# Token tables of the gates from two rounded one-hot products, with the low part of the gate made by ScalarE

## The chip, the cores and the metric

The kernel runs on one NeuronCore of a Trainium2 chip. TensorE (PE) multiplies, and its weight loads are shown as PEld; VectorE (DVE), ScalarE (ACT) and GpSimd (POOL) work beside it; SyncE (SP) issues most DMAs. Each engine runs its own list of instructions strictly in the order of the program and waits on semaphores where the program says so. The metric is the device time of one execution in microseconds (us), less is better.

## The reference

One transformer-like layer over 512 tokens of width 1024: a gated mix of attention and convolution, and then a retrieval (PEER) from a table of 128 x 128 = 16384 experts. All inputs are float32. The change lies in the second half:

```
q = (hf @ w_q).reshape(T, PEER_HEADS, 2, PEER_DHALF)
scores = einsum('thpd,pnd->thpn', q, sub_keys)          # 128 first and 128 second keys
sv, si = top_k(scores, 16)
cand = sv[:, :, 0, :, None] + sv[:, :, 1, None, :]
cv, ci = top_k(cand, 16)                                 # 8 heads x 16 = 128 slots a token
e_idx = si0[ia] * 128 + si1[ib]
gates = softmax(cv)
a = einsum('thkd,td->thk', u_tab[e_idx], x)
out = einsum('thk,thkd->td', gelu(a) * gates, v_tab[e_idx])
```

## The kernel before

The kernel does not gather the expert rows of three of its four tiles of 128 tokens. It multiplies all 16384 rows of `u_tab` with these 384 tokens (the first product, 128 chunks of 128 experts), takes gelu of everything, multiplies by a dense table of gates that is zero for experts a token did not choose, and multiplies by all of `v_tab` (the second product). Matrices are split into a rounded high part and a low part, both of type fp32r, and each product is three matmuls (`three`, lines 1785 to 1787): high by high, low weight by high, high weight by low.

The dense table of gates has one 128 x 128 matrix for each token: entry (second key, first key). For tile 1 it is filled by 128 scattering DMAs of GpSimd (line 727). For two further tiles (`LAID` = 2) it is made on chip, a token at a time, as a product of one-hot matrices over the token's 128 slots: `one_hots` (lines 1620 to 1635) makes for `WIDE` = 8 tokens at once, a set, a matrix that is 1 where the slot's first key equals the column, one for the second key, and multiplies the latter by the slot's gate. That is three DVE instructions of 128 x 1024 a set, 16 sets a tile. `token_gates` (line 2065) then issues a plain float32 matmul a token, four tokens to a group (`TOK` = 4), two groups to a set, into bank 2 or 3. The profile shows each such float32 matmul as two instructions, so a group as x8. ACT copies each bank into `stage` (`gates`, line 972), and every eighth copy a DMA writes `stage` to memory.

All of this is laid beside the first product. A step is one chunk of it: 8 units of three matmuls on PE. Tile by tile there are four stages of 14, 14, 26 and 26 steps (`STEPS`); the last two, which this text calls stage 3 and stage 4, carry the token tables of the two tiles. In them PE issues group b before unit `GATE_UNIT[b]`, that is from step 4 on, one every 5.5 units, 32 groups a stage; a set is used every 11 units, or 1.375 steps.

What each engine does in its order in one step:

- ACT (`selecting` at line 989, `ahead` at line 965): gelu of the chunk just multiplied (line 963), the high part `whi` of the chunk after the next (line 952, three buffers `SPL`), then the copies of those groups that belong to this step (line 981).
- DVE (`select`, line 1505): the search for the next tile (top 16, candidates, sums), and between its parts (`beside`) the low parts `wlo` of the chunks (line 1467) and the sets. The table `LOWS` says how many low parts come at each point, and a set comes before a low part as soon as `KD * (made[0] - 1) // 11` allows it.
- POOL: the scatters and, for a few chunks a stage (`SEARCHING`), the low part in place of DVE (line 717).
- PE: the first product of chunk c waits for its low part and for the gelu of chunk c - 2; a group waits for its set (`one_r`) and for the copy of the group two before it (`gt_sb`).

A set may overwrite its buffer once the groups of the set `BUFS` earlier are multiplied (`gt_mm`); there are four buffers of 8 KB.

Of the kernel before, what the change touches and what calls it, by code (L numbers as in the profile page):

```python
# [5 lines left out]
F32 = mybir.dt.float32  # L6
F32R = mybir.dt.float32r
I32 = mybir.dt.int32
U32 = mybir.dt.uint32
ALU = mybir.AluOpType  # L10
ACT = mybir.ActivationFunctionType
AX = mybir.AxisListType.X

P = 128
D = 1024
T = 512
KD = D // P
TT = T // P
# [8 lines left out]
NK = 128  # L27
# [60 lines left out]
WIDE = 8  # L88
# [65 lines left out]
LOWS = ((1, 1, 1, 1, 1, 1, 1, 1, 1, 1, 1, 1, 0, 1, 0, 1), (1, 3, 3, 2, 2, 2, 2, 1, 1, 1, 1, 1, 1, 1, 1, 3))  # L154

LAID = TD - 1
BUFS = 4
SEL_UNIT, GATE_LEAD = 12, 4
GATE_UNIT = [KD * GATE_LEAD + b * KD * (STEPS[2] - GATE_LEAD) // NBT for b in range(NBT)]
EXP_STEP = (11, 11, 22, 22)  # L160
# [6 lines left out]
def build(nc, x, cb, ccol, w_modn, b_modc, w_modt, wblk, b_fc, conv_wc, conv_vec, keys_t, u_t, u_tab, v_tab, rows, out):  # L167
    with ExitStack() as ctx:
# [3 lines left out]
        def sb(name, shape, dt, kb):  # L172
            return nc.alloc_sbuf_tensor_at(name, shape, dt, offset=base + int(kb * KB))

        def sem(name):
            return ctx.enter_context(nc.semaphore(name))

        bank = [ctx.enter_context(nc.psum_tensor(f"bank{i}", [P, 512], F32)) for i in range(8)]
# [46 lines left out]
        stage = sb("stage", [P, 2, NK, TB], F32, 120)  # L225
        eq = sb("eq", [P, 2, TOPK * NCAND], F32, 192)
        selT = sb("selT", [P, 3, P], F32, 199)
        one = [sb(f"one{i}", [P, 2, WIDE, NK], F32, 152 + 8 * i) for i in range(BUFS)]
        selS = sb("selS", [P, SLOTS], I32, 190)
        selW = sb("selW", [P, SLOTS], F32, 190.5)  # L230
        zeros = sb("zeros", [P, HALF], F32, 132)
# [157 lines left out]
        selT_mm = sem("selT_mm")  # L389
        selT_sb = sem("selT_sb")  # L390
        one_r = sem("one_r")
        zero_r = sem("zero_r")
        zero_out = sem("zero_out")
        gate_add = sem("gate_add")
# [30 lines left out]
        class Chain:  # L425
# [5 lines left out]
            def link(self, ins):  # L431
                self.n += 1
                ins.then_inc(self.s, 1)
                self.eng.wait_ge(self.s, self.n)
# [329 lines left out]
        def _(act):  # L764
# [45 lines left out]
            for n in range(G0):  # L810
                if n > 1:
                    hi(n + 2)
                if n >= Q0:
                    act.wait_ge(blk_mm, n + 1)
                    dst = qa if n < K0 else ka
                    for r in range(2):
                        ins = nc.scalar.activation(dst[0:DH, 2 * ((n - Q0) % 4) + r, :],
                                                   bank[z_bank[n]][r * DH:(r + 1) * DH, :], ACT.Copy,
                                                   scale=-DH ** -0.5 if n < K0 else 1.0)
# [145 lines left out]
            def ahead(c):  # L965

                if c:
                    gelu(c - 1)
                if c + 2 < CH:
                    part_u(c + 2)  # L970

            def gates(l, b):
# [11 lines left out]
                if t0 == TB - TOK:  # L984
                    act.wait_ge(gt_sb, n + 1)
                    act.dma_start(gates_dram[:, :, P // TB + blk, :],
                                  stage[:, s].rearrange("p (q f) t -> p q (f t)", f=4)).then_inc(stage_out[s], 16)

            def selecting(s):
                for j in range(STEPS[s]):  # L990
                    ahead(S_AT[s] + j)
                    if j == EXP_STEP[s]:
                        act.wait_ge(gate_sub, s + 1)
                        nc.scalar.activation(sel[:, 1, :, :], cv[:], ACT.Exp).then_inc(gate_exp, 1)
                    if s >= TT - LAID:
                        for b in range(NBT):
                            if GATE_UNIT[b] // KD == j:
                                gates(s - TT + LAID, b)
# [65 lines left out]
        def _(dve):  # L1064
# [544 lines left out]
            def transposed(s):  # L1609

                dve.wait_ge(selT_mm, s)
                nc.vector.tensor_copy(selT[:, 2, :], bank[2][:, P:2 * P])
                link(nc.vector.tensor_copy(selI[:, 0, :], bank[2][:, 0:P]))
                link(nc.vector.tensor_scalar(selI[:, 1, :], selI[:, 0, :], NK - 1, None, ALU.bitwise_and))
                link(nc.vector.tensor_scalar(selI[:, 0, :], selI[:, 0, :], NK.bit_length() - 1, None,
                                             ALU.logical_shift_right))
                link(nc.vector.tensor_copy(selT[:, 0:2, :], selI[:]))
                nc.vector.nop().then_inc(selT_sb, 1)

            def one_hots(l, o):  # L1620

                shape = [P, WIDE, NK]
                n = P // WIDE * l + o
                if n == 0:
                    dve.wait_ge(xs_r, 2)
                need(dve, gt_mm, 2 * (n - BUFS) + 2)
                row = one[n % BUFS]
                part = slice(o * WIDE, (o + 1) * WIDE)
                keys_of = iota[:].unsqueeze(1).broadcast_to(shape)
                link(nc.vector.tensor_tensor(row[:, 1], selT[:, 0, part].unsqueeze(2).broadcast_to(shape), keys_of,  # L1630
                                             ALU.is_equal))
                nc.vector.tensor_tensor(row[:, 0], selT[:, 1, part].unsqueeze(2).broadcast_to(shape), keys_of,  # L1632
                                        ALU.is_equal)
                nc.vector.tensor_tensor(row[:, 1], row[:, 1], selT[:, 2, part].unsqueeze(2).broadcast_to(shape),  # L1634
                                        ALU.mult).then_inc(one_r, 1)

            nc.vector.tensor_scalar(tokI[:, 1:2], tokI[:, 1:2], TB.bit_length() - 1, None, ALU.logical_shift_right)
# [142 lines left out]
        def _(pe):  # L1780
# [284 lines left out]
            def token_gates(l, b):  # L2065

                n = NBT * l + b
                pe.wait_ge(one_r, n // 2 + 1)
                need(pe, gt_sb, n - 1)
                if b == 0:  # L2070
                    pe.wait_ge(selT_sb, l + 1)
                row = one[n // 2 % BUFS]
                for j in range(TOK):
                    i = n % 2 * TOK + j
                    last = mm(bank[2 + b % 2][:, j * NK:(j + 1) * NK], row[:, 0, i, :], row[:, 1, i, :],  # L2075
                              start=True, stop=True)
                last.then_inc(gt_mm, 1)

            def selecting(s):
# [105 lines left out]
```

## Time and profile before

| | |
|---|---|
| median of three runs | 1624.3 us (1623.93 to 1624.91) |
| profiled execution, its own time | 1621.99 us |
| its span | 1620.2 us |
| PE busy, weight loads busy | 1554.3 us (96%), 1358.6 us (84%) |
| DVE, ACT, POOL busy | 1361.3 us (84%), 679.4 us (42%), 680.6 us (42%) |
| chain that ended last | PE 61%, DVE 26%, DMA 7%, issue 4%, ACT 1% |
| matmuls of the token tables (line 2075) | x512, 276 ns each |
| sets (lines 1630, 1632, 1634) | 32 of each, 1.2 us each where nothing disturbs |

Stage 3 lies between about 579 us and 725 us of the span (the transposes of line 2062 stand at 579.0 and 724.8 us), stage 4 behind it until about 862 us. Matmuls and ACT instructions overlap their neighbours, so the distance between two starts says what one costs, and its duration is longer than that. A wait is printed in brackets behind the instruction that waited, with the work that released it.

### The profile page before, as it was taken

How to read it: one execution, taken by the hardware profiler on the slowest of the kernel's cores; microseconds unless marked ns; L12 is line 12 of the kernel's file. 1: busy time of each engine (PE TensorE's matmuls, PEld its weight loads, DVE VectorE, ACT ScalarE, POOL GpSimd, SP SyncE). 2: the span in 40 equal slices, each digit the busy share in tenths (PEclk: the TensorE clock that was granted, in tenths of full speed). 3: DMA queues.
4: the chain of work that ended last, by engine and by line, in shares of the span. 5: the costliest groups of instructions: out<-in, count | busy, mean ns of one | idle time of the engine just before them, and what ended most of it. 6: DMA issues, size and time to landing. Idle time of an engine off the chain costs nothing.

```text
span 1620.2 us, 21549 instructions
## 1 busy us (share of the span) xinstructions
PE 1554.3 (96%) x7772; PEld 1358.6 (84%) x7772; DVE 1361.3 (84%) x2603; ACT 679.4 (42%) x923; POOL 680.6 (42%) x445
## 2 busy tenths in 40 slices
PE   5999999997999999999999999999999899999997
PEld 3888777776899999999999999999988688877775
DVE  6579887797288899979994888888878899999998
ACT  4344656435334344555554433333323333333341
POOL 0201000000043778777864455565553555555511
PEclk9999999998999999999999999999999999999998
DMA  9423444562367657686868999999989999999981
GB/s 365 145 90 118 130 130 130 195 208 78 119 228 251 170 146 182 153 236 169 217 183 285 411 395 350 373 356 365 342 296 372 401 409 409 409 409 408 409 328 52
DMA packets 162489, 422.17 MB, mean 261 GB/s; under 512 B 31568, under 2 KB 64464, under 8 KB 162128
## 3 DMA queue, kind: packets, MB, share of 16 engines
q1 hardware_dynamic: 72288, 264.44, 44.6%
q0 software_dynamic: 57200, 139.58, 25.4%
q10 hardware_dynamic: 32896, 16.78, 3.7%
q8 instruction: 62, 1.02, 0.2%
q14 instruction: 43, 0.35, 0.1%
HBM read 375.55 MB, written 45.15 MB: 260 GB/s over the span
## 4 chain that ended last, share of the span: by engine, by line
PE 61%; DVE 26%; DMA 7%; issue 4%; ACT 1%; SPq 0%; DVEq 0%; ACTq 0%
PE bank L1785 18%; PE bank L1787 18%; PE bank L1786 18%; DVE acc L1703 6%; DMA vraw<-in_v_tab_dram 6%; DVE one L1632 2%; DVE wf L1658 2%; DVE one L1630 2%; DVE wlo L1467 2%; DVE one L1634 2%; DVE el L1665 2%; PE bank L2075 1%; PE bank L1931 1%; PE bank L1916 1%; PE bank L2051 1%
## 5 line engine op out<-in xcount | busy, mean ns | idle before, releaser
L1785 PE MATMUL bank<-act_hi,whi 128*128 128x384 f32 (+1 forms) x1352 | 480.7, 356 | 3.6 <-DVE act_lo L1181 2.1
L1787 PE MATMUL bank<-act_hi,wlo 128*128 128x384 f32 (+1 forms) x1352 | 472.0, 349 | 0.0
L1786 PE MATMUL bank<-act_lo,whi 128*128 128x384 f32 (+1 forms) x1352 | 471.8, 349 | 0.0
L1785 PE MATMUL bank<-vhi,eh 128*128 128x512 f32 x768 | 302.6, 394 | 15.2 <-DVE el L1665 15.0
L1787 PE MATMUL bank<-vhi,el 128*128 128x512 f32 x768 | 301.3, 392 | 0.0
L1786 PE MATMUL bank<-vlo,eh 128*128 128x512 f32 x768 | 301.2, 392 | 0.0
L1785 PEld LDWEIGHTS bank<-act_hi,whi 128*128 128x128 f32 x1352 | 255.1, 189 | 20.6 <-DVE act_lo L1181 3.6
L1786 PEld LDWEIGHTS bank<-act_lo,whi 128*128 128x128 f32 x1352 | 255.2, 189 | 13.7
L727 POOL DMA_INDIRECT gates_by_key<-selW,selS x128 | 237.7, 1857 | 67.3 <-issue 46.3
L1787 PEld LDWEIGHTS bank<-act_hi,wlo 128*128 128x128 f32 x1352 | 254.7, 188 | 13.3
L750 POOL DMA_INDIRECT ring<-in_v_tab_dram,idxN x128 | 185.9, 1452 | 174.5 <-DVE acc L1703 136.3
L711 POOL DMA_INDIRECT ring<-in_u_tab_dram,idxN x128 | 178.0, 1391 | 150.8 <-DVE ring L1472 107.1
L1670 DVE TENSOR_TENSOR vlo<-vraw,vhi 128x1024 fp32r<-128x1024 f32 x128 | 156.2, 1221 | 65.7 <-ACT vhi L1024 65.4
L1024 ACT ACTIVATE vhi<-vraw 128x1024 fp32r<-128x1024 f32 x128 | 134.9, 1055 | 129.5 <-PE bank L1787 109.2
L1467 DVE TENSOR_TENSOR wlo<-raw,whi 128x1024 fp32r<-128x1024 f32 x108 | 131.9, 1222 | 66.5 <-ACT whi L952 66.0
L1785 PEld LDWEIGHTS bank<-vhi,eh 128*128 128x128 f32 x768 | 145.2, 189 | 50.7 <-issue 22.0
L1011 ACT ACTIVATE eh<-wf 128x384 fp32r<-128x384 f32 x128 | 67.4, 526 | 281.8 <-DVE wf L1658 275.9
L1787 PEld LDWEIGHTS bank<-vhi,el 128*128 128x128 f32 x768 | 145.2, 189 | 30.9
L1786 PEld LDWEIGHTS bank<-vlo,eh 128*128 128x128 f32 x768 | 145.3, 189 | 29.6 <-issue 0.2
L1703 DVE SCALAR_TENSOR_TENSOR acc<-ring,own_a,acc 128x1024 f32<-128x1024 f32 x127 | 162.7, 1281 | 5.4 <-DVE acc L1703 0.5
L1472 DVE SCALAR_TENSOR_TENSOR ring<-ring,x2s 128x1024 f32<-128x1024 f32 x128 | 149.9, 1220 | 0.7 <-DMA ring<-in_u_tab_dram,idxN 0.7
L963 ACT ACTIVATE gelz<-bank 128x384 f32<-128x384 f32 x128 | 63.3, 495 | 179.6 <-PE bank L1787 177.1
(256 smaller groups left out, 1964.7 us busy)
## 6 DMA issues: line engine op xcount, KB each, us to landing
raw<-in_u_t_dram SPq DMA_DIRECT2D x128, 512.0 KB, 7.2
vraw<-in_v_tab_dram SPq DMA_DIRECT2D x128, 512.0 KB, 10.8
raw<-in_wblk_dram SPq DMA_DIRECT2D x61, 512.0 KB, 4.4
gring<-gates_by_key SPq DMA_DIRECT2D x32, 768.0 KB, 12.0
raw<-in_w_modt_dram SPq DMA_DIRECT2D x32, 512.0 KB, 3.7
gates_by_key<-stage ACTq DMA_DIRECT2D x8, 2048.0 KB, 13.9
gelu_ahead<-gelz SPq DMA_DIRECT2D x20, 768.0 KB, 4.2
gback<-gelu_ahead SPq DMA_DIRECT2D x40, 384.0 KB, 17.7
```

What stands on the lines that cost most here:

```text
L711: pool.indirect_dma_start(out=ring[:, j % RING, :], out_offset=None, in_=u_tab, in_offset=bass.IndirectOffsetOnAxis(ap=idxN[:, j:j + 1], a ...
L727: pool.indirect_dma_start(out=gates_flat, out_offset=bass.IndirectOffsetOnAxis(ap=selS[:, n:n + 1], axis=0), in_=selW[:, n:n + 1], in_offs ...
L750: pool.indirect_dma_start(out=ring[:, j % RING, :], out_offset=None, in_=v_tab, in_offset=bass.IndirectOffsetOnAxis(ap=idxN[:, j:j + 1], a ...
L1011: nc.scalar.activation(e_parts(n)[0], wf[:, n % 2, :], ACT.Copy).then_inc(w_hi, 1)
L1024: nc.scalar.activation(v_parts(n)[0], row, ACT.Copy).then_inc(v_hi, 1)
L1467: nc.vector.tensor_tensor(wlo[:, c % SPL, :], raw[:, c % RAW, :], whi[:, c % SPL, :].bitcast(F32), ALU.subtract).then_inc(u_lo, 1)
L1472: nc.vector.scalar_tensor_tensor(out=ring[:, j % RING, :], in0=ring[:, j % RING, :], scalar=1.0, in1=x2s[:], op0=ALU.mult, op1=ALU.mult, a ...
L1670: nc.vector.tensor_tensor(low, v_row(n)[0], high.bitcast(F32), ALU.subtract).then_inc(v_lo, 1)
L1703: nc.vector.scalar_tensor_tensor(out=acc[:, TD, :], in0=ring[:, j % RING, :], scalar=own_a[:, j:j + 1], in1=acc[:, TD, :], op0=ALU.mult, o ...
L1785: mm(o, wh, mh, start=start, stop=False)
L1786: mm(o, wh, ml, start=False, stop=False)
L1787: return mm(o, wl, mh, start=False, stop=stop)
```

## The change

- DVE now writes the two one-hots of a set as fp32r (`one_a`, `one_b`), and a third tile `one_g`, the second one-hot times the high part of the gate. There are still three DVE instructions a set.
- ACT makes the fourth tile in place: `low_gates` multiplies `one_b` by the low part of the gate, one instruction of 128 x 128 for each of the 8 tokens, with the token's column of `selT` as a scale operand. It counts `one_lo`. It stands in ACT's order right after `ahead`, in the step before the one in which the set is first used.
- The high and the low part of the gates are made once a tile in `transposed`: a copy to fp32r and a subtraction in place of one copy.
- PE waits for `one_lo` in place of `one_r`, and issues two fp32r matmuls of 128 columns a token, which add up in the bank.
- A set is 12 KB in place of 8 KB, and there are two buffers in place of four.

```diff
-BUFS = 4
+BUFS = 2
...
+            def low_gates(l, o):
+                n = P // WIDE * l + o
+                act.wait_ge(one_r, n + 1)
+                for i in range(WIDE):
+                    token = o * WIDE + i
+                    last = nc.scalar.activation(one_b[n % BUFS][:, i, :], one_b[n % BUFS][:, i, :].bitcast(F32), ACT.Copy,
+                                                scale=selT[:, 2, token:token + 1])
+                last.then_inc(one_lo, 1)
+
             def selecting(s):
                 for j in range(STEPS[s]):
                     ahead(S_AT[s] + j)
+                    if s >= TT - LAID:
+                        for o in range(P // WIDE):
+                            if GATE_UNIT[2 * o] // KD - 1 == j:
+                                low_gates(s - TT + LAID, o)
...
-                nc.vector.tensor_copy(selT[:, 2, :], bank[2][:, P:2 * P])
+                link(nc.vector.tensor_copy(gate_hi[:], bank[2][:, P:2 * P]))
+                nc.vector.tensor_tensor(selT[:, 2, :], bank[2][:, P:2 * P], gate_hi[:].bitcast(F32), ALU.subtract)
...
                 need(dve, gt_mm, 2 * (n - BUFS) + 2)
-                row = one[n % BUFS]
...
-                link(nc.vector.tensor_tensor(row[:, 1], selT[:, 0, part].unsqueeze(2).broadcast_to(shape), keys_of,
+                link(nc.vector.tensor_tensor(one_b[n % BUFS][:], selT[:, 0, part].unsqueeze(2).broadcast_to(shape), keys_of,
                                              ALU.is_equal))
-                nc.vector.tensor_tensor(row[:, 0], selT[:, 1, part].unsqueeze(2).broadcast_to(shape), keys_of,
+                nc.vector.tensor_tensor(one_a[n % BUFS][:], selT[:, 1, part].unsqueeze(2).broadcast_to(shape), keys_of,
                                         ALU.is_equal)
-                nc.vector.tensor_tensor(row[:, 1], row[:, 1], selT[:, 2, part].unsqueeze(2).broadcast_to(shape),
+                nc.vector.tensor_tensor(one_g[n % BUFS][:], one_b[n % BUFS][:].bitcast(F32),
+                                        gate_hi[:, part].bitcast(F32).unsqueeze(2).broadcast_to(shape),
                                         ALU.mult).then_inc(one_r, 1)
...
-                pe.wait_ge(one_r, n // 2 + 1)
+                pe.wait_ge(one_lo, n // 2 + 1)
...
-                    last = mm(bank[2 + b % 2][:, j * NK:(j + 1) * NK], row[:, 0, i, :], row[:, 1, i, :],
-                              start=True, stop=True)
+                    mm(bank[2 + b % 2][:, j * NK:(j + 1) * NK], one_a[k][:, i, :], one_g[k][:, i, :], start=True, stop=False)
+                    last = mm(bank[2 + b % 2][:, j * NK:(j + 1) * NK], one_a[k][:, i, :], one_b[k][:, i, :],
+                              start=False, stop=True)
```

How the instructions stand on ACT at steps 3 to 6 of stage 3, before (gelz is a gelu, whi a high part, stage the copy of a group):

```order
L963 ACTIVATE gelz<-bank 128x384
L952 ACTIVATE whi<-raw 128x1024
L963 ACTIVATE gelz<-bank 128x384
L952 ACTIVATE whi<-raw 128x1024
L981 ACTIVATE stage<-bank 128x4x128 x2
L963 ACTIVATE gelz<-bank 128x384
L952 ACTIVATE whi<-raw 128x1024
L981 ACTIVATE stage<-bank 128x4x128
L963 ACTIVATE gelz<-bank 128x384
L952 ACTIVATE whi<-raw 128x1024
L981 ACTIVATE stage<-bank 128x4x128 x2
```

And now (the eights on one_b are the low parts of sets 0, 1 and 2):

```order
L967 ACTIVATE gelz<-bank 128x384
L956 ACTIVATE whi<-raw 128x1024
L998 ACTIVATE one_b_101<-one_b_101,selT 128x128 x8
L967 ACTIVATE gelz<-bank 128x384
L956 ACTIVATE whi<-raw 128x1024
L998 ACTIVATE one_b_102<-one_b_102,selT 128x128 x8
L985 ACTIVATE stage<-bank 128x4x128 x2
L967 ACTIVATE gelz<-bank 128x384
L956 ACTIVATE whi<-raw 128x1024
L998 ACTIVATE one_b_101<-one_b_101,selT 128x128 x8
L985 ACTIVATE stage<-bank 128x4x128
```

The low part of set 1 now stands ahead of the copies of the first two groups, and that of set 2 ahead of the copy of the third; nothing else moved.

On DVE the same place, after the change (two sets, a low part of a chunk, a part of the search, a set); before, the three rows of a set stand at the same places with `one` in place of the three names:

```order
L1647 TENSOR_TENSOR one_b_102<-selT,iota 128x1024
L1649 TENSOR_TENSOR one_a_100<-selT,iota 128x1024
L1651 TENSOR_TENSOR one_g_104<-one_b_102,gate_hi 128x1024
L1647 TENSOR_TENSOR one_b_101<-selT,iota 128x1024
L1649 TENSOR_TENSOR one_a_99<-selT,iota 128x1024
L1651 TENSOR_TENSOR one_g_103<-one_b_101,gate_hi 128x1024
L1484 TENSOR_TENSOR wlo<-raw,whi 128x1024
L1505 MATCH_REPLACE sc_94<-both_of,bank 128x128 x16
L1647 TENSOR_TENSOR one_b_102<-selT,iota 128x1024
```

The low part `wlo` right behind set 2 (the second set shown) is that of chunk 8 of the stage, whose high part ACT makes in step 6.

## Rows read from the trace of the kernel before

**Rows 1.** Part 1 of the page: engine, busy us, share, instructions.

```profile
PE 1554.3 (96%) x7772; PEld 1358.6 (84%) x7772; DVE 1361.3 (84%) x2603; ACT 679.4 (42%) x923; POOL 680.6 (42%) x445
```

**Rows 2.** Windows in stage 3: length, then busy of PE, PEld, DVE, ACT, POOL; clock.

```profile
592.00:640.00 48.00, 46.20 (x297) 45.28 (x296) 47.54 (x115) 25.23 (x29) 39.47 (x20) 1.00 0.65 175
640.00:690.00 50.00, 49.37 (x315) 48.63 (x315) 47.46 (x126) 24.63 (x28) 40.43 (x22) 1.00 0.69 164
690.00:724.00 34.00, 32.65 (x209) 32.33 (x208) 25.99 (x38) 19.91 (x24) 22.89 (x14) 1.00 0.84 241
```

**Rows 3.** Waits, 575 to 862 us: who for whom; total us, times, longest.

```profile
ACT stage L981 <- PE bank L2075: 82.9, 45, 5.1
DVE wlo L1467 <- ACT whi L952: 18.9, 11, 3.8
PEld bank L2075 <- DVE one L1634: 8.3, 8, 2.3
```

**Rows 4.** Timeline of PE around one group: start, us, engine, line, operands.

```profile
589.34 0.33 PE L1785 MATMUL bank<-act_hi,whi 128*128 128x384 f32 x1
589.69 0.33 PE L1787 MATMUL bank<-act_hi,wlo 128*128 128x384 f32 x1
589.86 1.05 PE L2075 MATMUL bank<-one 128*128 128x128 f32 x8
590.93 0.34 PE L1786 MATMUL bank<-act_lo,whi 128*128 128x384 f32 x1
```

**Rows 5.** Weight loads by form (count, busy, mean ns), and eight on the timeline.

```profile
L1787 PEld LDWEIGHTS bank<-act_hi,wlo 128*128 128x128 f32 x1352 | 254.7, 188 | 13.3
L1931 PEld LDWEIGHTS bank<-probT,vals 128*64 128x64 f32 x64 | 8.1, 136 | 12.8 <-issue 7.6 <-ACT probT L845 3.9
...
20.33 0.97 PEld L1881 LDWEIGHTS bank<-strips,mrows 128*128 128x128 f32 x8
```

**Rows 6.** Timeline of ACT in stage 3.

```profile
590.45 1.05 ACT L952 ACTIVATE whi<-raw 128x1024 fp32r<-128x1024 f32 x1
...
601.32 0.49 ACT L963 ACTIVATE gelz<-bank 128x384 f32<-128x384 f32 x1 [1.49 <-PE bank L1787]
601.71 1.05 ACT L952 ACTIVATE whi<-raw 128x1024 fp32r<-128x1024 f32 x1
602.65 1.13 ACT L981 ACTIVATE stage<-bank 128x512 f32<-128x512 f32 x1
```

**Rows 7.** ACT by form: count, busy, mean ns of one.

```profile
L952 ACT ACTIVATE whi<-raw 128x1024 fp32r<-128x1024 f32 x128 | 134.6, 1053 | 3.0 <-DMA raw<-in_u_t_dram 3.0
...
L1059 ACT ACTIVATE acc<-acc,sq 128x1024 f32<-128x1024 f32 x2 | 2.3, 1150 | 4.3 <-DVE sq L1110 4.3
...
L1051 ACT ACTIVATE own_a<-own_a 128x128 f32<-128x128 f32 x1 | 0.3, 294 | 0.0
```

**Rows 8.** Timeline of DVE: ends of sets 1 and 2, chunk 8, set 5.

```profile
596.23 1.22 DVE L1634 TENSOR_TENSOR one<-one,selT 128x1024 f32<-128x1024 f32 x1
...
601.84 1.21 DVE L1634 TENSOR_TENSOR one<-one,selT 128x1024 f32<-128x1024 f32 x1
602.98 1.21 DVE L1467 TENSOR_TENSOR wlo<-raw,whi 128x1024 fp32r<-128x1024 f32 x1
...
624.76 1.22 DVE L1630 TENSOR_TENSOR one<-selT,iota 128x1024 f32<-128x1024 f32 x1
...
628.29 1.22 DVE L1467 TENSOR_TENSOR wlo<-raw,whi 128x1024 fp32r<-128x1024 f32 x1
```

**Rows 9.** The transposes of line 2062: loads, ns, first and last start.

```profile
L2062 PEld LDWEIGHTS bank<-ident,sel x4: 138/140/143, 579.0 to 724.8; 128*128 128x128 f32 x4
```

**Rows 10.** PE in stage 4: a group that waited, the next; clock after it.

```profile
812.94 1.16 PE L2075 MATMUL bank<-one 128*128 128x128 f32 x8 [1.98 <-DVE one L1634]
...
818.11 1.05 PE L2075 MATMUL bank<-one 128*128 128x128 f32 x8
...
815.00:818.00 3.00, 3.00 (x12) 3.00 (x11) 2.93 (x4) 1.66 (x3) 1.25 (x2) 0.54 0.56 129
```

More of the change, by code:

```diff
@@ L227, in build @@
         selT = sb("selT", [P, 3, P], F32, 199)
-        one = [sb(f"one{i}", [P, 2, WIDE, NK], F32, 152 + 8 * i) for i in range(BUFS)]
+        gate_hi = sb("gate_hi", [P, P], F32R, 200.5)
+        one_a = [sb(f"one_a{i}", [P, WIDE, NK], F32R, 152 + 12 * i) for i in range(BUFS)]
+        one_b = [sb(f"one_b{i}", [P, WIDE, NK], F32R, 156 + 12 * i) for i in range(BUFS)]
+        one_g = [sb(f"one_g{i}", [P, WIDE, NK], F32R, 160 + 12 * i) for i in range(BUFS)]
         selS = sb("selS", [P, SLOTS], I32, 190)
@@ L391, in build @@
         one_r = sem("one_r")
+        one_lo = sem("one_lo")
         zero_r = sem("zero_r")
@@ L2071, in token_gates @@
                     pe.wait_ge(selT_sb, l + 1)
-                row = one[n // 2 % BUFS]
+                k = n // 2 % BUFS
                 for j in range(TOK):
                     i = n % 2 * TOK + j
-                    last = mm(bank[2 + b % 2][:, j * NK:(j + 1) * NK], row[:, 0, i, :], row[:, 1, i, :],
-                              start=True, stop=True)
+                    mm(bank[2 + b % 2][:, j * NK:(j + 1) * NK], one_a[k][:, i, :], one_g[k][:, i, :], start=True, stop=False)
+                    last = mm(bank[2 + b % 2][:, j * NK:(j + 1) * NK], one_a[k][:, i, :], one_b[k][:, i, :],
+                              start=False, stop=True)
                 last.then_inc(gt_mm, 1)
```

## The prediction

> **What bounds the kernel now.** I read the page's busy times first [rows 1]: PE is busy 96% of the span, DVE 84%, ACT only 42%. By these shares work for ACT looks free and time saved on PE looks worth having. But the change lies in stages 3 and 4 alone, so I read windows of stage 3 next [rows 2]. From 592 to 690 us PE is busy 95.6 of 98 us, DVE 95.0, ACT 49.9: PE and DVE are both full there, and whoever is helped alone gains nearly nothing. Only from 690 us on has DVE idle time (8.0 of 34 us). The waits come third [rows 3]: PE's weight loads waited 8 times for a set of one-hots (8.3 us in the two stages), so sets arrive just in time, and DVE waited for high parts 11 times, most of it at the ends of stages. ACT sits idle 83 us in front of the copies of groups. That is the trap: it is idle because it stands in its order and waits, and what it does next is wanted by DVE (the high parts) and by PE (gelu and copies). The last view is the timelines of the three engines about sets 1 and 2, with the order in which the instructions stand.
>
> **PE: two rounded products for a float32 one.** A group costs what it pushes apart its neighbours [rows 4]: 590.93 - 589.69 = 1.24 us between starts that are otherwise two spacings of 0.173 us apart (589.34 to 589.69), so 0.893 us for 8 instructions, 112 ns each. It stays 8 instructions: before two for each float32 product, now two products. No row shows an fp32r matmul of 128 columns. The line through its widths would be 0.173 us less 256 columns at 2.4 GHz (107 ns), 67 ns, or 0.53 us a group. But each has its own weights, and a load of 128 columns lasts 188 ns against 136 ns for 64, so 52 ns for 64 columns and some 105 ns for 128 [rows 5]. Eight loads whose matmuls have a single column start (0.97 - 0.19) / 7 = 111 ns apart [rows 5]. So I take 112 ns again, nothing gained. Below, 67 ns would give 64 groups x 0.36 = 23 us of PE's time back. Above, I take twice the price, 64 x 0.89 = 57 us more of it.
>
> The Trainium skill (TensorE: Matmul & The Clock Gate, section Back-to-back issue gap) says that a stream of load and matmul pairs at 128 columns runs at about 81 ns each. By that a group would be 0.65 us and PE would have 64 x 0.24 = 16 us less to do; the eight loads at 111 ns speak against it.
>
> **DVE.** Three instructions of 128 x 1024 a set before and after; rounded output costs the same (1.21 to 1.22 us for wlo, which is fp32r, and for one, [rows 8]), and a set with its hand-offs takes 628.29 - 624.76 = 3.5 us. `transposed` gets one small instruction more, some 0.3 us twice, which has the first steps of a stage as cover. Two buffers in place of four: set n now waits for the second group of set n - 2. From there to the first group of set n PE has 16.5 units of 0.52 us and two groups, 10.4 us, and set plus low part need 5.8 us. No cost; at worst a few of the waits below change their name.
>
> **ACT: the low part of the gate.** 32 sets x 8 instructions of 128 x 128. An instruction of that size lasts 294 ns, one with a column as scale about 95 ns more (1150 against 1053 at 1024 wide) [rows 7], and starts of neighbours are some 110 ns closer than a duration (601.71 to 602.65 is 0.94 for one of 1.05) [rows 6]: 0.28 us each, 2.3 us a set, 73 us in all. Bounds: 0.18 us each if the scale costs nothing (1.5 us a set), 0.39 if nothing overlaps (3.1). As busy time it fits: 1.375 steps take PE 5.7 us and two groups 1.8, so 7.5 us; ACT has in them 1.375 x (0.4 + 0.94) for gelu and high part, 2 x 1.1 for copies, and now 2.3: 6.3 us.
>
> **What is behind the new wait.** ACT must have the finished set one step before PE uses it, and sets are finished when PE uses it. Set 1 is ready at 596.23 + 1.22 = 597.45 us [rows 8], and ACT is through with the high part ahead of it at 591.5 [rows 6]. Behind its wait stand the copies of groups 0 and 1, gelu, and the high part of chunk 7. With the durations above: low part of set 1 until 599.8, two copies until 601.9, gelu 602.3, high part 603.3, low part of set 2 (ready at 603.05 [rows 8]) until 605.6, copy of group 2 606.7, gelu 607.1, high part of chunk 8 at 608.1. DVE wants exactly that right behind set 2, at 602.98 [rows 8]. It stands still 5.1 us, and DVE is an engine that has no time to give. PE meanwhile waits for the copy of group 0 before group 2.
>
> That is a circle: DVE ends a set, ACT does low part (2.3), one copy (1.1), gelu (0.4) and high part (1.0), 4.9 us with hand-offs, and only then can DVE do the low part of the chunk that stands before its next set. Where the chunk behind a set is the third after ACT's step, all of it is a stall; where ACT's step comes later or the search stands between, part of it. I followed the order of the four engines through both stages so, each instruction starting at the end of its engine's last or of what it waits for. For the kernel before this gives 148 and 144 us for the two stages (the transposes at the heads of stages 3 and 4 stand 724.8 - 579.0 = 145.8 us apart [rows 9]) and nearly no stall of DVE in mid-stage. After the change DVE stalls, in stage 3, at chunks 8, 11, 12, 16, 18, 19, 22 and 23 for 5.1, 3.2, 4.9, 1.5, 2.2, 4.9, 2.9 and 4.9 us, 29.6 in all; in stage 4 at chunks 8, 11, 12, 18, 19, 22 and 23 for 5.1, 1.9, 4.9, 2.2, 4.9, 2.9 and 4.9, 26.8. To each stage comes 3.1 us in which the search waits for its exponential, which ACT now reaches late, and 2.1 us at the stage's end. Stage 3 grows by 34.8, stage 4 by 32.0 us: 67 us.
>
> The size of it hangs on the low part: 23 us for each us of a set's 2.3 (49 us in all at 1.5, 86 at 3.1). It hardly hangs on PE, since PE now waits anyway: 0.53 us a group takes off only 2 us, 1.8 us adds 8. After stage 4 all work stands behind PE's last groups as before, and I pass on the whole.
>
> **Clock.** PE will wait some 19 times for 2 to 6.5 us where it had one such wait. After that one, of 1.98 us, the granted clock was 0.54 from 815 to 818 us, which is the lower level of 1.2 GHz for nearly all of it, and the next group came 5.17 us later, where the undisturbed ones are 5 x 0.52 + 0.89 = 3.49 apart [rows 10]: 1.7 us. Most such slow stretches end in PE's next wait and cost nothing. I take 4 us (bounds 0 and 19 x 1.7 = 32).
>
> **Sum.** 1622.0 (the profile's own time) + 0 (PE) + 0 (sets, buffers) + 67 + 4 = 1693 us. The median of the runs is 2.3 us above the profile's time, so 1695 on the scale of the runs.
>
> **Rivals.**
> 1. Only a delay. DVE has the low parts far enough ahead and the chain through ACT moves PE later once a stage, by low part and copy, 3.4 us: 1624.3 + 7 = 1631. For it: ACT has busy time to spare [rows 2]. Against it: the low part of chunk 8 follows set 2 with no gap [rows 8], so there is no lead. 12%.
> 2. A narrow fp32r matmul is slow on top of the circle, twice the price or more: 1695 + 8 = 1703, and at four times the price a group takes 3.6 us, PE needs 26 x 4.16 + 3.5 + 32 x 3.6 = 227 us a stage in place of some 180, and it would be about 1790. For it: no row is narrower than 384 columns. Against it: the width of 384 runs at 160 ns for its columns and 13 more, with no sign of a step. 10%.
> 3. Faster. If a set were ready a step before its use everywhere, ACT's wait would be free, and PE would gain up to 0.36 us a group. Its place is where DVE has idle time, the last six groups of each stage (12 x 0.36 = 4.3 us) and DVE's 3 us of idle in mid-stage: 1624.3 - 7 = 1617. It decides from a lead of the sets over their groups of one step, 5 us; rows 3 and 8 show leads of nothing. 5%.
> 4. The new operand is cheaper than its bounds, or ACT's waits end earlier than I follow them, so that half the growth comes: 1655 to 1665. 8%.
>
> **Chances.** My forecast, the circle, has 65%, between 1672 (low part 1.5 us, no clock) and 1722 (3.1 us and 10 for the clock). The range 1655 to 1725 takes in rival 4 and the first half of rival 2. What this kernel's runs can tell from no change is about 0.2%, 3 us. Faster by more 4%, within it 3%, slower 93%.
>
> **What would show it.** In the profile after: ACT waiting for DVE's third instruction of a set, a line that is not there now, at some 25 to 30 sets; DVE waiting in front of wlo for whi some 25 times in place of 11, together about 75 us in place of 18.9; eight low parts in about 2.3 us; PE idle 12 to 18% of stages 3 and 4 and its clock below 1.00 there; the two transposes of line 2062 some 180 us apart in place of 145.8. It would be wrong if that distance stayed under 150 us, if PE itself were busy longer with the groups (start to start over 1.4 us for eight), or if the growth lay behind stage 4.

## The result: 70 us slower, and the profile after

The changed kernel takes 1694.4 us (median of four runs, 1693.5 to 1694.9) against 1624.4, a ratio of 1.0432 (95% interval 1.0419 to 1.0445). The forecast was 1695, with a range of 1655 to 1725.

First the page after, its busy times, and the windows of stage 3 that answer to [rows 1] and [rows 2]:

```profile
PE 1577.7 (93%) x7772; PEld 1376.6 (81%) x7772; DVE 1356.7 (80%) x2605; ACT 744.6 (44%) x1179; POOL 670.5 (40%) x445
```

```profile
592.00:640.00 48.00, 39.60 (x239) 38.68 (x238) 33.97 (x94) 27.04 (x58) 30.16 (x16) 0.93 0.51 146
640.00:690.00 50.00, 42.77 (x256) 41.45 (x255) 36.88 (x140) 30.68 (x63) 38.44 (x22) 0.93 0.60 135
690.00:724.00 34.00, 28.23 (x166) 27.00 (x165) 26.09 (x29) 18.44 (x38) 24.52 (x14) 0.95 0.51 117
```

ACT is still the least busy of the three, at 57.7 of 98 us between 592 and 690, and yet PE fell there from 95.6 to 82.4 us and DVE from 95.0 to 70.9. All three wait now. The waits say for whom (answering to [rows 3]; who for whom, us in total, times, longest; 575 to 935 us):

```profile
ACT one_b L998 <- DVE one_g L1651: 97.9, 25, 7.4
DVE wlo L1484 <- ACT whi L956: 88.9, 26, 6.8
...
PE bank L2093 <- ACT stage L985: 36.1, 13, 5.9
...
PE bank L2093 <- ACT one_b L998: 18.5, 7, 5.0
```

ACT waits for DVE's sets and DVE for ACT's high parts, 98 and 89 us in the same two stages: two engines in a circle. PE waits for the copies of groups and for the low parts, 20 times and 54.6 us in all, which is 16% of the two stages.

One turn of it, on ACT's timeline in stage 3 after the change:

```profile
593.29 1.05 ACT L956 ACTIVATE whi<-raw 128x1024 fp32r<-128x1024 f32 x1
600.33 2.44 ACT L998 ACTIVATE one_b<-one_b,selT 128x128 fp32r<-128x128 f32 x8 [6.00 <-DVE one_g L1651]
602.68 1.90 ACT L985 ACTIVATE stage<-bank 128x512 f32<-128x512 f32 x2
604.38 0.53 ACT L967 ACTIVATE gelz<-bank 128x384 f32<-128x384 f32 x1
604.79 1.06 ACT L956 ACTIVATE whi<-raw 128x1024 fp32r<-128x1024 f32 x1
605.74 2.46 ACT L998 ACTIVATE one_b<-one_b,selT 128x128 fp32r<-128x128 f32 x8
608.08 1.10 ACT L985 ACTIVATE stage<-bank 128x512 f32<-128x512 f32 x1
608.95 0.55 ACT L967 ACTIVATE gelz<-bank 128x384 f32<-128x384 f32 x1
609.38 1.07 ACT L956 ACTIVATE whi<-raw 128x1024 fp32r<-128x1024 f32 x1
```

and DVE's, which answers to [rows 8] (end of set 2, then chunk 8):

```profile
602.61 1.22 DVE L1651 TENSOR_TENSOR one_g<-one_b,gate_hi 128x1024 fp32r<-128x1024 f32 x1
610.48 1.23 DVE L1484 TENSOR_TENSOR wlo<-raw,whi 128x1024 fp32r<-128x1024 f32 x1 [6.65 <-ACT whi L956]
```

ACT waits 6.00 us for set 1, and after that everything that stood behind it runs without a gap: low part, two copies, gelu, high part, low part of set 2, a copy, gelu, and at 610.45 the end of the high part of chunk 8 that DVE has wanted since 603.83. DVE then loses 6.65 us where it lost none before.

The stages by their transposes, answering to [rows 9]:

```profile
L2080 PEld LDWEIGHTS bank<-ident,sel x4: 138/140/142, 581.6 to 763.6; 128*128 128x128 f32 x4
```

182.0 us from one to the next in place of 145.8: stage 3 grew by 36.2. From the last transpose to the start of the last token matmul it is 928.8 - 763.6 = 165.2 in place of 856.7 - 724.8 = 131.9: stage 4 grew by 33.3. Stage 3 also starts 2.6 us later than in the profile of before; the kernels of the experiments, which are the same up to there but for their buffers, start it between 579.4 and 581.5, so I do not count that as the change's. The three make 72.1 of the 72.4 us between the two spans. Behind stage 4 nearly nothing was gained or lost (0.3 us).

### The profile page after: what moved, and what is told of

The parts are those of the page before. It is cut to its first block, busy times and chain, and to the rows that moved or that the text cites. A ratio compares the mean times of both kernels' runs of the same rounds, so it can differ in the third digit from the quotient of the medians.

```text
span 1692.6 us, 21807 instructions
## 1 busy us (share of the span) xinstructions
PE 1577.7 (93%) x7772; PEld 1376.6 (81%) x7772; DVE 1356.7 (80%) x2605; ACT 744.6 (44%) x1179; POOL 670.5 (40%) x445
## 4 chain that ended last, share of the span: by engine, by line
PE 55%; DVE 26%; ACT 7%; DMA 6%; issue 5%; SPq 0%; DVEq 0%; ACTq 0%
PE bank L1803 17%; PE bank L1804 17%; PE bank L1805 16%; DVE acc L1721 7%; DMA vraw<-in_v_tab_dram 6%; ACT one_b L998 3%; DVE wf L1676 2%; DVE one_b L1647 2%; DVE one_a L1649 2%; DVE one_g L1651 2%; DVE el L1683 2%; DVE wlo L1484 1%; ACT stage L985 1%; ACT whi L956 1%; PE bank L1949 1%
## 5 line engine op out<-in xcount | busy, mean ns | idle before, releaser
L1804 PE MATMUL bank<-act_lo,whi 128*128 128x384 f32 (+1 forms) x1352 | 477.2, 353 | 0.0
L1803 PEld LDWEIGHTS bank<-act_hi,whi 128*128 128x128 f32 x1352 | 259.4, 192 | 20.6 <-DVE act_lo L1198 2.6
L1804 PEld LDWEIGHTS bank<-act_lo,whi 128*128 128x128 f32 x1352 | 258.9, 192 | 13.6
L1805 PEld LDWEIGHTS bank<-act_hi,wlo 128*128 128x128 f32 x1352 | 258.6, 191 | 13.5
L731 POOL DMA_INDIRECT gates_by_key<-selW,selS x128 | 231.8, 1811 | 64.3 <-issue 45.5
L1484 DVE TENSOR_TENSOR wlo<-raw,whi 128x1024 fp32r<-128x1024 f32 x108 | 131.9, 1222 | 137.9 <-ACT whi L956 137.3
L956 ACT ACTIVATE whi<-raw 128x1024 fp32r<-128x1024 f32 x128 | 134.3, 1051 | 6.4 <-DMA raw<-in_u_t_dram 6.4
```

The source lines that it names most:

```text
L731: pool.indirect_dma_start(out=gates_flat, out_offset=bass.IndirectOffsetOnAxis(ap=selS[:, n:n + 1], axis=0), in_=selW[:, n:n + 1], in_offs ...
L956: nc.scalar.activation(whi[:, c % SPL, :], raw[:, c % RAW, :], ACT.Copy).then_inc(u_hi, 1)
L1484: nc.vector.tensor_tensor(wlo[:, c % SPL, :], raw[:, c % RAW, :], whi[:, c % SPL, :].bitcast(F32), ALU.subtract).then_inc(u_lo, 1)
L1803: mm(o, wh, mh, start=start, stop=False)
L1804: mm(o, wh, ml, start=False, stop=False)
L1805: return mm(o, wl, mh, start=False, stop=stop)
```

## The experiments

All were timed beside the kernel before on the same chip.

**Two buffers.** The kernel before with one number changed:

```diff
-BUFS = 4
+BUFS = 2
```

> The kernel before with two buffers of one-hots in place of four, nothing else. Theory (the circle DVE set, ACT low part, copy, gelu, high part, DVE low part makes the growth): no change, 1624 within 3 us, since a set's buffer is free 10.4 us before its next use. Rival (the missing buffers hold DVE back, and the circle is only where it shows): a clear part of the 70 us, 1640 or more, with DVE waiting for the groups of PE ahead of line 1630.

1624.05 us, ratio 1.000 (0.999 to 1.0009). Two buffers cost the kernel before nothing.

**No low part.** The changed kernel without its ACT instructions:

```diff
-                    if s >= TT - LAID:
-                        for o in range(P // WIDE):
-                            if GATE_UNIT[2 * o] // KD - 1 == j:
-                                low_gates(s - TT + LAID, o)
...
-                pe.wait_ge(one_lo, n // 2 + 1)
+                pe.wait_ge(one_r, n // 2 + 1)
```

> The changed kernel without the low parts on ACT: the second product takes the second one-hot as it is, so the gate's low part is left out and the one-hot stands in its place; PE waits for the set again. All else stays: two fp32r matmuls a token, two buffers of 12 KB. Theory: PE's price is unchanged at 112 ns an instruction and all of the growth hangs on ACT's part, so 1624 within 4 us. Rival (fp32r matmuls of 128 columns cost more on PE): 8 us or more above, 1632 to 1640. Rival (they are cheaper, 67 ns): PE has time to spare in stages 3 and 4, up to 7 us below, 1617.

1624.38 us, ratio 1.0001 (0.9991 to 1.001). PE in this kernel, around a group:

```profile
591.36 0.33 PE L1801 MATMUL bank<-act_hi,wlo 128*128 128x384 f32 x1
591.54 0.22 PE L2089 MATMUL bank<-one_g,one_a 128*128 128x128 f32 x1
591.60 0.27 PE L2090 MATMUL bank<-one_b,one_a 128*128 128x128 f32 x1
591.71 0.27 PE L2089 MATMUL bank<-one_g,one_a 128*128 128x128 f32 x1
...
592.61 0.34 PE L1800 MATMUL bank<-act_lo,whi 128*128 128x384 f32 x1
```

592.61 - 591.36 = 1.25 us, less two spacings of 0.173 makes 0.90 us a group, against 0.893 in [rows 4]. The fp32r pair costs PE what the float32 matmul cost. So the whole of the growth hangs on ACT's part and on the wait for it.

**One wide instruction.** The changed kernel with ACT's eight instructions made one:

```diff
-                for i in range(WIDE):
-                    token = o * WIDE + i
-                    last = nc.scalar.activation(one_b[n % BUFS][:, i, :], one_b[n % BUFS][:, i, :].bitcast(F32), ACT.Copy,
-                                                scale=selT[:, 2, token:token + 1])
+                last = nc.scalar.activation(one_b[n % BUFS][:], one_b[n % BUFS][:].bitcast(F32), ACT.Copy, scale=2.0 ** -13)
```

> The changed kernel with the eight ACT instructions of a set made one of 128 x 1024 with a constant scale, so all tokens get the same factor in place of their gate's low part; 0.95 us a set in place of 2.45. Theory: the circle stays, each full stall of DVE shrinks by 1.5 us; from the same order of the engines followed through the stages 41 us remain of 70, so 1665 (1658 to 1672). Rival (it is ACT's added work that counts, 78 us then, 30 us now): 1651. Rival (a delay once a stage): 1629.

1666.66 us, ratio 1.0253 (1.0236 to 1.027): 42.4 us above before. The theory's 41 is met, the 27 that ACT's added work alone would give and the 5 of a mere delay are not. ACT waits as long for the sets as with the full low part:

```profile
ACT one_b L996 <- DVE one_g L1648: 103.7, 29, 7.4
DVE wlo L1481 <- ACT whi L956: 82.3, 33, 7.0
```

These rows run to 935 us, but the last token matmul of this kernel starts at 900.6, and behind stage 4 DVE waits for high parts in the kernel before too. From the first transpose to the last token matmul DVE waits for high parts 62.4 us in 24 waits, against 83.9 in 23 in the changed kernel and 14.9 in 9 before. So about a quarter of DVE's waiting went, as it should where each turn of the circle is 1.5 us shorter.

**Sets earlier.** The changed kernel with one number of DVE's order changed:

```diff
-                        while lays >= 0 and made[1] < min(P // WIDE, KD * (made[0] - 1) // 11):
+                        while lays >= 0 and made[1] < min(P // WIDE, KD * made[0] // 11):
```

> The changed kernel with each set made one low part earlier in DVE's order (KD * made // 11 in place of KD * (made - 1) // 11), nothing else; ACT does all its low parts at the same places. Theory: ACT finds the sets ready or nearly so, DVE no longer waits for high parts in mid-stage, and most of the growth goes: 1628 (1624 to 1640). Rival (ACT's 78 us of added work, or the hand-over as such, is the price): stays at 1680 to 1695. Rival (two buffers are then too few, DVE waits for groups): 1645 to 1660.

1625.51 us, ratio 1.0008 (0.9998 to 1.0018). All of ACT's 256 instructions are there, at the same places, and the growth is gone but for 1.3 us, which is within the noise. Its timeline of ACT shows how:

```profile
591.54 1.05 ACT L956 ACTIVATE whi<-raw 128x1024 fp32r<-128x1024 f32 x1
592.49 2.44 ACT L998 ACTIVATE one_b<-one_b,selT 128x128 fp32r<-128x128 f32 x8
594.83 2.01 ACT L985 ACTIVATE stage<-bank 128x512 f32<-128x512 f32 x2
```

The low part of set 1 starts right behind the high part, without the wait of 6.00 us that it had. ACT still waits for sets, but 41.0 us in 14 waits in place of 97.9 in 25, and DVE waits for high parts 13.5 us in 6 waits within the two stages, in place of 83.9 in 23: the circle is open. Two buffers suffice here too: PE's groups hold up DVE for 4.0 us in all.

**Copies first.** The changed kernel with ACT's low parts behind the copies of the same step:

```diff
                     ahead(S_AT[s] + j)
-                    if s >= TT - LAID:
-                        for o in range(P // WIDE):
-                            if GATE_UNIT[2 * o] // KD - 1 == j:
-                                low_gates(s - TT + LAID, o)
...
                         for b in range(NBT):
                             if GATE_UNIT[b] // KD == j:
                                 gates(s - TT + LAID, b)
+                        for o in range(P // WIDE):
+                            if GATE_UNIT[2 * o] // KD - 1 == j:
+                                low_gates(s - TT + LAID, o)
```

> The changed kernel with ACT's low parts behind the copies of the same step in place of ahead of them, nothing else. Theory: the copies that PE waits for come first, but the high part of the next step still stands behind the low part and its wait, so the circle stays: 54 us above before by the same following of the order, 1678 (1668 to 1688). Rival (it is the copies held back that make the growth): 1640 or less. Rival (place within the step is nothing): 1694.

1687.6 us, ratio 1.0388 (1.0374 to 1.0402): 63 us above, not 54. The copies held back explain little, the circle is what counts, as the theory had it; but I had this order 10 us too good: the time lies at the edge of my range and nearer to the rival's 1694 than to my 1678, so the place within the step is worth 7 us and not 16. PE now waits 28 times for the low part itself, 49.2 us, where it waited 7 times and 18.5 us:

```profile
DVE wlo L1483 <- ACT whi L956: 83.5, 26, 7.8
...
PE bank L2092 <- ACT one_b L998: 49.2, 28, 5.2
```

**High part only.** The changed kernel without the low part (the edit of the run without it) and without the second product:

```diff
-                    mm(bank[2 + b % 2][:, j * NK:(j + 1) * NK], one_a[k][:, i, :], one_g[k][:, i, :], start=True, stop=False)
-                    last = mm(bank[2 + b % 2][:, j * NK:(j + 1) * NK], one_a[k][:, i, :], one_b[k][:, i, :],
-                              start=False, stop=True)
+                    last = mm(bank[2 + b % 2][:, j * NK:(j + 1) * NK], one_a[k][:, i, :], one_g[k][:, i, :],
+                              start=True, stop=True)
```

> The changed kernel with neither ACT's low parts nor the second product, so the low part of each gate is left out: four fp32r matmuls a group in place of eight instructions. Theory: PE gets back 64 x 0.45 = 29 us of work, but DVE is full in the same stages, so only 3 to 7 us show: 1619 (1616 to 1622). Rival (PE bounds the stages): 1596.

1623.88 us, ratio 0.9999 (0.999 to 1.0008). Even the 3 to 7 us that I granted do not show, although PE has some 29 us less to do (64 groups of 0.45 us, an estimate). PE waits instead, and for the sets:

```profile
PE bank L2089 <- DVE one_g L1647: 23.0, 12, 5.8
```

In the kernel before the same row of PE (`bank L2075` waiting for `one L1634`) has 5.8 us in 5 waits; among the weight loads it is 26.8 us in 12 against the 8.3 in 8 of [rows 3]. With the sets where they stand, PE waits for DVE, and less work on PE buys nothing. But part of the work saved was eaten by the clock: the mean granted clock of both stages is 0.95 in this kernel, where it was 1.00 and 0.99, and PE's busy time in them fell from 271.9 to 255.4 us only, by 16.5 and not 29. Whether the 3 to 7 us were lost by the waits alone or also by the clock is not separated.

**ACT's gates.** If ACT can take eight small instructions a set, it can take them from DVE. The kernel before, in float32 and with four buffers, where ACT does the multiplication by the gate and the sets come one low part earlier:

```diff
+                act.wait_ge(one_r, n + 1)
...
+                    last = nc.scalar.activation(one[n % BUFS][:, 1, i, :], one[n % BUFS][:, 1, i, :], ACT.Copy,
+                                                scale=selT[:, 2, token:token + 1])
+                last.then_inc(one_lo, 1)
...
-                        while lays >= 0 and made[1] < min(P // WIDE, KD * (made[0] - 1) // 11):
+                        while lays >= 0 and made[1] < min(P // WIDE, KD * made[0] // 11):
...
-                                        ALU.is_equal)
-                nc.vector.tensor_tensor(row[:, 1], row[:, 1], selT[:, 2, part].unsqueeze(2).broadcast_to(shape),
-                                        ALU.mult).then_inc(one_r, 1)
+                                        ALU.is_equal).then_inc(one_r, 1)
...
-                pe.wait_ge(one_r, n // 2 + 1)
+                pe.wait_ge(one_lo, n // 2 + 1)
```

> The kernel before (float32 one-hots, one matmul a token, four buffers), with DVE's third instruction of a set moved to ACT: eight instructions of 128 x 128 that multiply the second one-hot by the token's gate, one step ahead of their use, and each set made one low part earlier. Theory: DVE, which is full in mid-stage, is rid of 32 x 1.14 = 36 us, ACT finds its sets ready, and stages 3 and 4 shrink to what PE needs, 26 x 4.16 + 3.5 + 32 x 0.89 = 140 us in place of 145.8: 1624 - 11 = 1613 (1608 to 1619). Rival (PE was the bound of these stages all along and its few waits come from elsewhere): 1622 to 1626. Rival (the hand-over through ACT costs by itself, as in the changed kernel): 1640 or more.

1614.84 us, ratio 0.994 (0.9926 to 0.9953): it beats both kernels. Its windows, to be held against [rows 2]:

```profile
592.00:640.00 48.00, 48.00 (x315) 48.00 (x314) 39.35 (x134) 41.32 (x87) 39.10 (x19) 1.00 0.66 182
640.00:690.00 50.00, 50.00 (x324) 49.59 (x323) 42.46 (x115) 39.39 (x79) 39.99 (x24) 1.00 0.70 176
```

PE is busy all of the time, DVE 82 of 98 us and ACT 81. The transposes stand 721.5 - 580.9 = 140.6 us apart, where PE alone needs 140. Which of the two edits did that, the next run shows.

**Earlier sets alone, and ACT's gates alone.** The two halves of that kernel, each by itself. First the kernel before with only this:

```diff
-                        while lays >= 0 and made[1] < min(P // WIDE, KD * (made[0] - 1) // 11):
+                        while lays >= 0 and made[1] < min(P // WIDE, KD * made[0] // 11):
```

> The kernel before with each set made one low part earlier, nothing else. Theory: it separates the two edits of the kernel that has ACT's gates and earlier sets. PE's waits for sets (8.3 us in the two stages) shrink, but DVE stays as full as it was: 1624 - 3 = 1621 (1618 to 1624). Rival (earlier sets alone are what gains): 1613.

1619.47 us, ratio 0.9971 (0.9961 to 0.9982): 4.8 us of the 9.4 come from the earlier sets. DVE's order alone was worth half, and the stages say where:

| | stage 3 | stage 4 |
|---|---|---|
| kernel before | 145.8 us | 131.9 us |
| earlier sets alone | 140.6 us | 132.2 us |
| earlier sets and ACT's gates | 140.6 us | 127.5 us |

(Stage 3 from transpose to transpose, stage 4 from the transpose to the last token matmul.) In stage 3 the earlier sets alone bring all of the gain: PE is busy from 592 to 690 us without a break there too, although DVE is busy for 97.0 of the 98 us. ACT's gates pay in stage 4: with earlier sets alone DVE is busy for 127.5 of its 132.2 us, and PE's weight loads wait 6 times, 4.2 us, for DVE's low parts; with ACT's gates DVE is busy for 104.1 of 127.5 us and PE for all of them.

This run also gives the changed kernel with earlier sets its right measure. It stands 1.3 us above the kernel before, but 1625.5 - 1619.5 = 6.0 us above the kernel before with the same earlier sets (the kernel before took 1624.2 and 1624.3 beside the two), 5.8 of them in stage 3 (146.4 against 140.6 us). So the hand-over is not free with the lead that this order gives it. PE's waits for copies, 7.8 us in 10, are a likely part of that; no run tests it.

Then the kernel with ACT's gates, with that line put back as it was before.

> The kernel with ACT's float32 gates, but the sets where the kernel before has them, one low part later; it has neither fp32r one-hots nor two products nor two buffers. Theory: the circle through ACT makes the growth whatever ACT's eight instructions are for, less than in the changed kernel since DVE is rid of a third of a set: 43 us by following the order, 1667 (1655 to 1680). Rival (the growth needs the changed kernel's other parts): 1615 to 1625, as with earlier sets.

1666.59 us, ratio 1.0269 (1.025 to 1.0287), 43 us above, as followed from the order. It has float32 one-hots, one product a token and all four buffers, and the circle is there (575 to 905 us, as its last token matmul starts at 900.0):

```profile
DVE wlo L1481 <- ACT whi L953: 100.2, 34, 8.1
ACT one L995 <- DVE one L1646: 69.9, 20, 6.2
```

It differs from the kernel with ACT's gates and earlier sets by that one line, and the same work takes some 52 us less there.

## Why the prediction was right, step by step

- **PE.** Nothing gained, forecast at 112 ns an instruction. Right: 0.90 us a group against 0.893. A short distance, near the 67 ns of the line through the wider forms, exists only once a group, at its head (591.54 to 591.60), where the weights of the first were loaded under the matmul of 384 columns ahead. From then on the loads of the run without the low part start 0.11 us apart (591.54, 591.65, 591.76), and each matmul 0.06 us behind its own load. The Trainium skill (TensorE: Matmul & The Clock Gate, section Back-to-back issue gap) gives about 81 ns for such a pair; the trace does not agree, it shows 112 ns.
- **DVE and buffers.** No cost forecast, none found (1624.05 us with two buffers; three instructions of some 1.22 us a set in the changed kernel as before).
- **ACT's instructions.** 0.28 us each and 2.3 us a set forecast; eight take 2.45 us. They last 387 ns each and start some 0.29 us apart. By the prediction's own slope, 23 us for each us, the 0.15 us more a set would have made the circle 3 us dearer.
- **The circle.** Forecast 34.8 and 32.0 us, with 4 for the clock, for the two stages; measured 36.2 and 33.3. DVE's waits for high parts rose from 18.9 us to 88.9 (forecast 75), their number from 11 to 26 (25). The turn at sets 1 and 2 was worked out as a stall of 5.1 us at chunk 8 and was 6.65. ACT's chain was as forecast, 10.15 us from set 1's end at 600.30 to the high part's end at 610.45 (10.65 in the prediction). But DVE ended set 2 only 3.5 us behind set 1, not 5.6 as before, because no instruction of set 2 was stretched this time (the last section has the stretched one). What DVE gained there it lost waiting.

  The whole of stage 3, by DVE, before and after:

```profile
579.00:724.80 145.80, 142.02 (x901) 140.01 (x900) 133.02 (x312) 74.99 (x87) 112.90 (x60) 1.00 0.71 184
...
581.60:763.60 182.00, 153.01 (x900) 148.96 (x900) 129.29 (x313) 108.07 (x215) 115.60 (x63) 0.93 0.57 145
```

  DVE's idle time grew from 12.8 to 52.7 us, by 39.9, and its work shrank by 3.7; that is the 36.2. The idle time is nine stalls in mid-stage of 2.0 to 6.7 us, 38.7 in all, where I had eight and 29.6 (the kernel before had one, of 2.0); a wait of the search for its exponential of 2.2 us where I had 3.1; and 1.5 us more at the stage's end where I had 2.1. The work shrank since the instructions of the sets, which last up to 3.9 us where they fall on POOL's own low parts, took 120.8 us in the two stages in place of 127.3. So the stalls were forecast 7 us too small, and the shorter work and the smaller waits give 5 of them back. In stage 4 there were eight stalls, 30.9 us, where I had seven and 26.8. The mechanism is the one forecast, but that the sum came within 1 us of the measured time is in part luck: it is better than its terms.
- **After stage 4.** Passed on whole, as forecast, within 0.3 us.
- **Clock.** The row that answers to [rows 10] is a wait of 5.00 us, and then

```profile
655.78 0.47 PE L2093 MATMUL bank<-one_g,one_a 128*128 128x128 f32 x1 [5.00 <-ACT one_b L998]
...
655.00:658.00 3.00, 2.22 (x10) 2.22 (x11) 2.92 (x4) 2.98 (x7) 2.70 (x2) 0.50 0.35 23
658.00:661.00 3.00, 3.00 (x12) 3.00 (x11) 2.93 (x14) 3.00 (x9) 2.70 (x2) 0.59 1.01 298
```

  The granted clock was at its lower level of 1.2 GHz until about 660.5 us. The mean clock of both stages is 0.93 where it was 1.00 and 0.99. PE had 20 waits where I had 19, but only ten of them were of 2 us or more. PE's busy time in the two stages rose from 271.9 to 292.4 us with the same number of instructions; how much of these 20.5 us ended in PE's next wait, and so cost nothing, no run separates. The 4 us stay an estimate: nothing shows them.
- **The rivals.** "Only a delay" (1631) and "half the growth" (1655 to 1665) are refuted by the time itself, and the delay by the wide instruction too. A cost of about the delay's size, 6.0 us, is left when the sets come earlier and the circle is open. The slow narrow matmul is refuted by the run without the low part. "Faster" named the right condition, a lead of the sets over their use: with it the changed kernel is level with before, but since PE's price did not fall it gains nothing, and with the same lead the kernel before is 6.0 us faster.
- **The signs.** PE idle 16% of the two stages (forecast 12 to 18), ACT's new wait 25 times (25 to 30), the transposes 182 us apart (180): all were met.
- **A sum.** The ends 1672 and 1722 of the forecast come to 1673 and 1720 by the terms given beside them (1624.3 + 49, and 1624.3 + 86 + 10). Nothing hangs on it.

## What to carry to other kernels

An engine's low busy share says nothing of what a new wait on it costs: read which instructions stand behind the wait in its order, and whether one of them is wanted by the engine it waits for. Where two engines hand work to each other in turn, each hand-over needs a lead, and moving the producer's instructions by one place can be worth more than the work itself: 69 us in the changed kernel and some 52 with ACT's gates, where the circle stood, but only 5 in the kernel before, which has no circle. Before giving the credit to an edit, run its halves: in stage 3 the earlier sets alone did all that both edits did. Price a cheaper number format by what bounds the instruction, here the load of its weights, one every 0.11 us.

## What the runs showed of the hardware that I had not expected

- An fp32r matmul of 128 columns with new weights starts 112 ns after the last (run without the low part, 591.60 to 592.38 for seven distances), the same as half of a float32 one (0.893 us for eight in the kernel before). Only one whose weights were loaded under a long matmul follows at some 60 ns (591.54 to 591.60).
- Taking an estimated 29 us of work off PE, the busiest engine, changed the time by 0.4 us, within the noise. PE waited more, the mean granted clock of the two stages was 0.95 in place of 1.00 and 0.99, and PE's busy time fell by 16.5 us only.
- A DVE instruction of 1.2 us can take 3.4 us. In the changed kernel with earlier sets:

```profile
599.77 3.41 DVE L1651 TENSOR_TENSOR one_g<-one_b,gate_hi 128x1024 fp32r<-128x1024 f32 x1
```

  In the kernel before such ones fall together with POOL's subtractions:

```profile
597.53 3.30 POOL L717 TENSOR_TENSOR wlo<-raw,whi 128x1024 fp32r<-128x1024 f32 x1 [1.04 <-ACT whi L952]
...
598.62 3.31 DVE L1632 TENSOR_TENSOR one<-selT,iota 128x1024 f32<-128x1024 f32 x1
```

  The DVE instruction starts inside POOL's and ends 601.93 - 600.83 = 1.10 us after it. In all six such pairs of the kernel before, and in the one of the changed kernel with earlier sets (603.18 - 602.09), it is 1.09 to 1.10 us, about what an undisturbed one takes, as if DVE had begun its work when POOL was through. That it is POOL's instructions that hold DVE up was not tried.
